# DVE's loads of expert numbers, POOL's fetches and the buffers of rows in two mixture-of-experts stages

## The reference

```python
def expert_block(args):
    xb, e = args
    hb = jax.nn.silu(xb @ w_gate[e]) * (xb @ w_up[e])
    return hb @ w_down[e]
```

## Time and profile before

| | |
|---|---|
| median of runs | 3517.16 us |
| profiled execution | 3516.36 us, span 3514.6 us |
| busy share of PE, DVE, ACT, POOL | 86%, 52%, 35%, 22% |
| mean granted clock of PE | 0.94 |
| DMA, mean over the span | 161 GB/s |

### The profile page before, as it was taken

How to read it: one execution, slowest core, us unless ns; L and a number is a source line. 1 busy time by engine, 2 the same in 40 slices (tenths; PEclk the granted TensorE clock), 3 DMA queues, 4 the chain that set the end, 5 groups by cost and what they waited for, 6 DMA issues and landing times. The chain is left out here.

```text
span 3514.6 us, 53911 instructions
## 1 busy us (share of the span) xinstructions
PE 3017.9 (86%) x17215; PEld 1423.1 (40%) x17216; DVE 1823.9 (52%) x2802; ACT 1212.8 (35%) x1768; POOL 761.8 (22%) x908
## 2 busy tenths in 40 slices
PE   8999999988999994788869997987888888888882
PEld 4444445545665443222247773444222222222220
DVE  3322224456774124333456674344677676776775
ACT  2221223334552001111133330211565555555564
POOL 1100000000000000434520000000555555555551
PEclk9999999998999996889979998999999999999996
DMA  6310021123221105888630101122778998888875
GB/s 227 125 66 30 0 102 49 54 57 84 73 73 60 68 36 201 332 346 347 225 142 25 36 27 66 63 102 104 268 242 290 333 331 277 304 286 274 281 236 180
DMA packets 188175, 564.40 MB, mean 161 GB/s; under 512 B 25340, under 2 KB 103776, under 8 KB 150912
## 3 DMA queue, kind: packets, MB, share of 16 engines
q1 hardware_dynamic: 146576, 425.10, 32.0%
q0 software_dynamic: 36528, 125.21, 13.6%
q10 hardware_dynamic: 4968, 12.74, 0.9%
HBM read 462.12 MB, written 100.86 MB: 160 GB/s over the span
## 5 line engine op out<-in xcount | busy, mean ns | idle before, releaser
L1467 POOL DMA_INDIRECT moe_xb<-token_rows,moe_idx x400 | 438.5, 1096 | 106.5 <-issue 93.0
L2137 DVE COPY h<-w_gu 128x1024 f32 (+1 forms) x342 | 267.0, 781 | 279.0 <-issue 238.7
L1561 POOL COPY moe_idx<-moe_slot_idx 128x4 int32<-128x4 int32 x4 | 0.6, 187 | 1814.6 <-DVE moe_slot_idx L1740 1814.6
L2030 PE MATMUL y_ps<-w_dn,hid_t 128*32 (+1 forms) x768 | 348.7, 597 | 11.1 <-issue 8.9
L2035 PE MATMUL y_ps<-h,hid_t 128*32 128x512 f32 (+1 forms) x768 | 348.7, 597 | 0.0
L362 PE MATMUL front<-second,wcol 128*128 128x512 f32 x768 | 332.1, 595 | 4.8 <-ACTq L68 2.4
L1999 PE MATMUL gu_ps<-w_gu,scores_mask 128*32 x576 | 278.8, 641 | 41.9 <-DVE more L2137 26.6
L2055 ACT ACTIVATE second<-w_gu 128x2048 f32 x146 | 271.0, 1903 | 98.6 <-issue 62.6
L1999 PE MATMUL gu_ps<-w_gu,more 128*32 x576 | 263.0, 611 | 48.7 <-DVE more L2125 16.3
L2004 PE MATMUL gu_ps<-second,scores_mask 128*32 128x512 f32 x576 | 278.9, 641 | 0.0
L2004 PE MATMUL gu_ps<-h,scores_mask 128*32 128x512 f32 x576 | 278.9, 641 | 0.0
(11 more groups left out here) (496 smaller groups left out, 6251.0 us busy)
## 6 DMA issues: line engine op xcount, KB each, us to landing
w_gu<-in_w_gate_dram SPq DMA_DIRECT2D x96, 1024.0 KB, 7.1
w_gu<-in_w_up_dram SPq DMA_DIRECT2D x96, 1024.0 KB, 11.0
w_dn<-in_w_down_dram SPq DMA_DIRECT2D x96, 1024.0 KB, 10.1
wcol<-in_w_in_dram SPq DMA_DIRECT2D x12, 1024.0 KB, 5.2
qk_by_head<-stage SPq DMA_DIRECT2D x32, 384.0 KB, 4.1
qk<-qk_by_head SPq DMA_DIRECT2D x16, 768.0 KB
expert_rows<-h ACTq DMA_DIRECT2D x24, 512.0 KB, 2.7
w_gu<-in_w_in_dram SPq DMA_DIRECT2D x20, 512.0 KB, 4.6
```

The source lines that it names most:

```text
L1467: g.indirect_dma_start(G.xb[:, slot % G.xb.shape[1], a, :], None, pieces, bass.IndirectOffsetOnAxis(ap=G.idx[:, slot, a:a + 1], axis=0)).t ...
L1561: g.tensor_copy(G.idx[:, b, :], G.slot_idx[:, b, :]).then_inc(idx_ready, 1)
L2030: nc.tensor.matmul(y_ps[0:SIZE, cs], hid_t[:, c, 0:SIZE], w_dn[:, bass.ds(ws, 1), c, cs].rearrange("p o n -> p (o n)"), start=c == 0, stop ...
L2137: d.tensor_copy(st_gu[a][:, :, cs, :], w_gu[:, bass.ds(ws, 1), :, cs, :].rearrange("p o g c n -> p (o g) c n")).then_inc(g_staged, 1)
```

## The change

Three things. DVE's step loads the expert numbers of block i+1 once and waits for their weights before it waits for `gu_ready`. POOL's iteration i now has `gather(i+2)` in front of `scatter(i-2)`, in both mixtures. And mixture 1 has two buffers for gathered rows and one for turned rows (instead of one and two): DVE turns the rows of block i+1 right behind `hid` of block i, since the one buffer is free only then; the dispatch stage gathers two blocks there, as it did for mixture 2. Cut to its core:

```diff
@@ dispatch, gpsimd
-            for b in range(G.xb.shape[1]):
+            for b in range(2):
                 gather_quads(g, G, rows_d, b)
@@ experts
         if more is None:
-            x_t = [rows.rearrange("p (c n) -> p c n", c=C) for rows in (work[:, 0], work[:, 1])]
+            x_t = [rows.rearrange("p (c n) -> p c n", c=C) for rows in (work[:, 0],)]
...
+        XT = len(x_t)
@@ experts, gpsimd
             def gather(b, slot):
-                pool.wait_ge(x_ready, b + 1 - XB)
+                pool.wait_ge(x_ready, b - 1)
                 if not by_slot:
-                    pool.wait_ge(share_ready, b + 1 - XB)
+                    pool.wait_ge(share_ready, b - 1)
...
-            for i in range(XB - 1, 4):
-                gather(i + 1, (i + 1) % 2)
+            for i in range(4):
+                gather(i + 2, i % 2)
                 if not by_slot and i >= 2:
                     scatter(i - 2, i % 2, None, 16 if i == 3 else None)
...
                     within.enter_context(pool.If(i <= n))
-                    gather(i + 1, 1 - u % 2)
+                    gather(i + 2, u % 2)
                     if not by_slot:
                         scatter(i - 2, u % 2, rounds + 16, rounds + (16 + 16 * (u % 2)))
@@ experts, vector
-            def stage_gate_up(b, pieces):
-                es = [v.value_load(G.blk_e[0:1, a, bass.ds(b, 1)], min_val=0, max_val=E - 1) for a in on_dve]
-                v.wait_ge(g_ready, es[-1] + 1)
-                if not (isinstance(b, int) and b == 0):
-                    v.wait_ge(gu_ready, b)
+            def experts_of(b):
+                return [v.value_load(G.blk_e[0:1, a, bass.ds(b, 1)], min_val=0, max_val=E - 1) for a in on_dve]
+
+            def stage_gate_up(es, pieces):
                 slots = [e % W for e in es]
...
             def step(i, turn, rounds):
                 slot = turn % 2
+                es = experts_of(i + 1)
+                v.wait_ge(g_ready, es[-1] + 1)
                 v.wait_ge(gu_ready, i + 1)
-                stage_gate_up(i + 1, (0,))
+                stage_gate_up(es, (0,))
                 v.wait_ge(silu_done, i + 1)
                 d.tensor_tensor(hid[:], act_g[:], gu_ps[:, slot, 1, :], ALU.mult).then_inc(hid_ready, 1)
-                stage_gate_up(i + 1, range(1, PIECES))
+                if XT == 1:
+                    v.wait_ge(x_in[1 - slot], (i + 1) // 2 * 64 + 64 if isinstance(i, int) else rounds * 4 + 128)
+                    turn_x(1 - slot)
+                stage_gate_up(es, range(1, PIECES))
                 stage_down(i)
-                v.wait_ge(x_in[slot], i // 2 * 64 + 128 if isinstance(i, int) else rounds * 4 + (128 + 64 * (1 - slot)))
-                turn_x(slot)
+                if XT == 2:
+                    v.wait_ge(x_in[slot], i // 2 * 64 + 128 if isinstance(i, int) else
+                              rounds * 4 + (128 + 64 * (1 - slot)))
+                    turn_x(slot)
@@ moe_state
-    G.xb = sb(f"moe_xb{E}", [P, lanes // 2, QUADS, width])
+    G.xb = sb(f"moe_xb{E}", [P, 2, QUADS, width])
@@ program
-            with nc.sbuf_tensor("work_1", [P, 2, D], F32) as work:
+            with nc.sbuf_tensor("work_1", [P, 1, D], F32) as work:
```

More of the change, by code:

```diff
@@ L1466, in gather_quads @@
     for a in range(QUADS):
-        g.indirect_dma_start(G.xb[:, slot % G.xb.shape[1], a, :], None, pieces, bass.IndirectOffsetOnAxis(
+        g.indirect_dma_start(G.xb[:, slot, a, :], None, pieces, bass.IndirectOffsetOnAxis(
             ap=G.idx[:, slot, a:a + 1], axis=0)).then_inc(G.xb_in[slot], 16)
@@ L1812, in experts @@
         xb, idx, mark = G.xb, G.idx, G.mark
-        XB = xb.shape[1]
         act_g = ph.sb("act_g", [P, F_EXP])
@@ L1921, in gather @@
             def gather(b, slot):
-                pool.wait_ge(x_ready, b + 1 - XB)
+                pool.wait_ge(x_ready, b - 1)
                 if not by_slot:
-                    pool.wait_ge(share_ready, b + 1 - XB)
+                    pool.wait_ge(share_ready, b - 1)
                 g.tensor_copy(idx[:, slot, :], G.slot_idx[:, bass.ds(b, 1), :].rearrange("p o a -> p (o a)")).then_inc(
                     idx_ready, 1)
-                pool.wait_ge(idx_ready, 2 * b + (1 - 2 * XB))
+                pool.wait_ge(idx_ready, 2 * b - 3)
                 g.tensor_tensor(mark[:, slot:slot + 1], G.tok[:, 0:1], G.tok[:, 0:1], ALU.add).then_inc(idx_ready, 1)
@@ L1974, in _ @@
                 pool.wait_ge(y_out_last, 16)
-            pool.wait_ge(x_in[0], (n + 3) // 2 * (16 * QUADS))
-            pool.wait_ge(x_in[1], (n + 2) // 2 * (16 * QUADS))
+            pool.wait_ge(x_in[0], (n + 4) // 2 * (16 * QUADS))
+            pool.wait_ge(x_in[1], (n + 3) // 2 * (16 * QUADS))
             if not by_slot:
-                pool.wait_ge(x_ready, n + 2)
+                pool.wait_ge(x_ready, n + XT)
                 pool.wait_ge(share_ready, n + 1)
@@ L1998, in step @@
                         pe.wait_ge(act_g_staged, 2 * i + (c * 2 // C + 1))
-                    nc.tensor.matmul(gu_ps[0:SIZE, slot], x_t[slot][:, c, 0:SIZE],
+                    nc.tensor.matmul(gu_ps[0:SIZE, slot], x_t[slot % XT][:, c, 0:SIZE],
                                      w_gu[:, bass.ds(ws, 1), :, c, :].rearrange("p o g n -> p (o g) n"),
@@ L2003, in step @@
                         at = slice(a * SIZE, (a + 1) * SIZE)
-                        last = nc.tensor.matmul(gu_ps[at, slot], x_t[slot][:, c, at], st_gu[a][:, :, c, :],
+                        last = nc.tensor.matmul(gu_ps[at, slot], x_t[slot % XT][:, c, at], st_gu[a][:, :, c, :],
                                                 start=c == 0, stop=c == C - 1)
@@ L2071, in take_share @@
                     e = a.value_load(G.blk_e[0:1, k, bass.ds(b, 1)], min_val=0, max_val=E - 1)
-                    last = s.activation(share[at, turn:turn + 1], xb[at, turn % XB, k, bass.ds(e + SUB, 1)], ACT.Copy)
+                    last = s.activation(share[at, turn:turn + 1], xb[at, turn % 2, k, bass.ds(e + SUB, 1)], ACT.Copy)
                 last.then_inc(share_ready, 1)
@@ L2124, in turn_x @@
             def turn_x(slot):
-                d.transpose(x_t[slot].rearrange("p c (a j) -> p a c j", j=QUARTER),
-                            xb[:, slot % XB, :, 0:SUB].rearrange("p a (i c) -> p a c i", c=C)).then_inc(x_ready, 1)
-            def stage_gate_up(b, pieces):
-                es = [v.value_load(G.blk_e[0:1, a, bass.ds(b, 1)], min_val=0, max_val=E - 1) for a in on_dve]
-                v.wait_ge(g_ready, es[-1] + 1)
-                if not (isinstance(b, int) and b == 0):
-                    v.wait_ge(gu_ready, b)
+                d.transpose(x_t[slot % XT].rearrange("p c (a j) -> p a c j", j=QUARTER),
+                            xb[:, slot, :, 0:SUB].rearrange("p a (i c) -> p a c i", c=C)).then_inc(x_ready, 1)
+            def experts_of(b):
+                return [v.value_load(G.blk_e[0:1, a, bass.ds(b, 1)], min_val=0, max_val=E - 1) for a in on_dve]
+            def stage_gate_up(es, pieces):
                 slots = [e % W for e in es]
@@ L2140, in stage_down @@
             def stage_down(b):
-                es = [v.value_load(G.blk_e[0:1, a, bass.ds(b, 1)], min_val=0, max_val=E - 1) for a in on_dve]
+                es = experts_of(b)
                 v.wait_ge(d_ready, es[-1] + 1)
@@ L2149, in step @@
                 slot = turn % 2
+                es = experts_of(i + 1)
+                v.wait_ge(g_ready, es[-1] + 1)
                 v.wait_ge(gu_ready, i + 1)
-                stage_gate_up(i + 1, (0,))
+                stage_gate_up(es, (0,))
                 v.wait_ge(silu_done, i + 1)
                 d.tensor_tensor(hid[:], act_g[:], gu_ps[:, slot, 1, :], ALU.mult).then_inc(hid_ready, 1)
-                stage_gate_up(i + 1, range(1, PIECES))
+                if XT == 1:
+                    v.wait_ge(x_in[1 - slot], (i + 1) // 2 * 64 + 64 if isinstance(i, int) else rounds * 4 + 128)
+                    turn_x(1 - slot)
+                stage_gate_up(es, range(1, PIECES))
                 stage_down(i)
-                v.wait_ge(x_in[slot], i // 2 * 64 + 128 if isinstance(i, int) else rounds * 4 + (128 + 64 * (1 - slot)))
-                turn_x(slot)
-            stage_gate_up(0, range(PIECES))
-            for b in range(2):
+                if XT == 2:
+                    v.wait_ge(x_in[slot], i // 2 * 64 + 128 if isinstance(i, int) else
+                              rounds * 4 + (128 + 64 * (1 - slot)))
+                    turn_x(slot)
+            es = experts_of(0)
+            v.wait_ge(g_ready, es[-1] + 1)
+            stage_gate_up(es, range(PIECES))
+            for b in range(XT):
                 v.wait_ge(x_in[b], 64)
@@ L2174, in moe_state @@
         G.m = sb(f"moe_m{E}", [P, T, E])[:]
-    G.slot_idx = sb(f"moe_slot_idx{E}", [P, NB + 5, QUADS], I32)[:]
+    G.slot_idx = sb(f"moe_slot_idx{E}", [P, NB + 6, QUADS], I32)[:]
     G.slot_row = sb(f"moe_slot_row{E}", [P, NB + 5], I32)[:] if lanes == 4 else None
```

## The result

The kernel after takes **3310.9 us** (median of 4 runs, 3308.1 to 3313.8) against 3517.5 for the one before on the same chip: ratio 0.9415, 95% interval 0.9398 to 0.9431. The profiled execution took 3308.1 us (span 3306.0).

The account below looks back on a forecast made before the run. DVE's late start behind register loads was taken to bound mixture 2, the only gather buffer mixture 1; -100 - 30 + 1 (additional gather) + 1.5 (tail) = -127.5 us, from 3517 to 3389 us, range 3335 to 3450.

Parts of the forecast that it names:

- term of -100 us for mixture 2: Mixture 2: mean period falls from 13.66 to 12.25 us over 71 blocks, DMA share then 0.93, -100 us.
- term of -30 for mixture 1: Mixture 1: second gather buffer removes the wait for rows, DMA then limits at a share of 0.94, -30 us.
- PE's floor is reached: Rival, both mixtures: DMA queues full at 0.98, -141 us in mixture 2, -45 in mixture 1, 3333 us; chance 0.18.
- PE's own period: Gate/up 7.07, hid's turn +3.37, next gate/up 0.96 to 1.40 later: 11.4 to 11.8 us a block at full clock.
- cap on DMA: Mixture 2: DMA engines busy 832 us; at 0.98 throughout the stage takes 849 us, a gain of 141; at 0.90, 66.
- signs of being wrong: Mixture 2: DVE's turns wait over 3 us for rows, loads over 1 us before the first copy, or DMA share stays 0.84.
- the 15 us that go by that rule: Mixture 1: at about 358 GB/s of HBM its 110 MB need 307 us, making the gain some 15 us smaller.
- the loads stay in the way: Rival: loads grow beside POOL's descriptor work, 1.5 of 2.78 us stays; -50 and -20 us, 3447 us; chance 0.10.
- Fetches are stretched by DVE's copies: Rival: POOL's gather issues slow beside DVE copies, gathers 5.3 us later; -47 and -25 us, 3445 us; chance 0.13.
- POOL ends last: Rival, slower: POOL's chain with five issues stretched by 1.3 us sets 15.2 us a block, +80 us, 3597; chance 0.04.
- later start of mixture 1: Before mixture 1: POOL issues four more gathers in front of the stage, so it starts 5 us later.
- the tail: End of mixture 2: a gather for a nonexistent block delays the last but one scatter, 0 to 6.2 us, taken as +1.5.

Follow-up runs that it names:

- number 8: Kernel after, but inside both mixture stages only the first half of each expert's down matrix is loaded: 3262.6 us, 0.9294 of before.
- number 7: Kernel after, but odd blocks' sums go into another table, so no scatter waits for the one before it: 3298.2 us, 0.9393 of before.
- number 1: Kernel before with only DVE's loads and wait for weights put in front of its wait for gate/up: 3438.0 us, 0.9788 of before.
- number 2: Kernel before with only mixture 2's gather put in front of the scatter, loads still behind the wait: 3414.6 us, 0.9722 of before.
- number 6: Kernel before, but in mixture 2 POOL holds each scatter, and the gather behind it, until the next gate/up ends: 3582.0 us, 1.0202 of before.
- number 5: Kernel before, but mixture 2's scatters, except the last, write rows instead of adding them: 3451.3 us, 0.984 of before.

## Why the prediction fell short

**The step that failed is the term of -100 us for mixture 2**: a mean period of 12.25 us, taken between PE's 11.6 and before with a DMA share of 0.93. Measured are 11.47 and -156 us. The term of -30 for mixture 1 was too small too, measured -48. No rival went as low either: "PE's floor is reached" had 3333. Two premises of the term were wrong, PE's own period and the cap on DMA. Of the prediction's signs of being wrong only single cases came (one turn that waited 5.8 us for rows, two of DVE's loads of over 1 us), and the DMA share rose to 0.95: the mechanism held, its size didn't.

**PE's own period: "7.07 + 3.37 + (0.96 to 1.40) = 11.4 to 11.8 us".** Measured are 10.87 in most of those 41 blocks of mixture 2, and 11.10 to 11.17 in 12 of mixture 1. The last term was read from a block in which hid came late and from one in which it came earlier, but not early enough. Once hid is ready, PE's sequencer sends hid's turn on to PE and then has register work for the next gate/up, the load of L1990 first. In the block of the earlier trace rows (before), and in the block shown after:

```profile
L1990 PEldq TENSOR_LOAD <-moe_blk_e x1: 298/298/298, 2907.7 to 2907.7; - x1
```
```profile
L1990 PEldq TENSOR_LOAD <-moe_blk_e x1: 298/298/298, 2600.4 to 2600.4; - x1
```

Both follow hid's end by 0.2 to 0.3 us. Before, the turn starts then too (2907.51), and the gate/up 1.40 behind it. After, the turn starts only behind the y products, at 2601.66, while the load of L1990 has begun at 2600.4: the register work goes on beneath the products, and the gate/up follows at +0.44. So the gap is near the larger of 3.80 and F + 3.1: blocks after with F of 1.41, 2.06 and 4.41 have gaps of 4.52, 5.15 and 7.50, a block before with 3.10 has 6.24 (a few lie up to 0.7 higher). Below an F of 0.7 nothing more is to be had, and that is where PE's period is 10.87. I had taken 1.40 (and 0.96) for PE's own; they were the exposed part of work that an early hid hides.

**The cap on DMA.** I held "832 us busy" for fixed work and chose 12.25 between PE and before, DMA share 0.93. After, the same bytes (335 GB/s x 823 us = 276 MB; before 280 x 990 = 277) took 0.95 x 823 = 782 busy us, 50 less. And a share can exceed 1 (1.02 over 200 us of mixture 1), so it sums the times of packets that overlap. It can't be divided by 0.98 to a floor: that gave 849 us for the stage, which took 814 from first to last gate/up. 11.47 lies inside what I had held for PE's own range; that is luck, since it is made of 10.87 in the undisturbed blocks and 0.6 on average of disturbance, mostly rows that come late. What is left above the floor is 71 x (11.47 - 10.87) = 43 us; number 8 gave back 29 of them, number 7 some 15.

**Mixture 1.** Forecast: last gate/up at 1709, -31; it came at 1692.7, -48. I took DMA at 0.94 (375 GB/s); it held 1.02 at 416 GB/s over 200 us. The Trainium skill's page "DMA: Bandwidth & Descriptors", section Specifications, gives about 358 GB/s of HBM for a core; here it doesn't hold over 200 of the stage's 288 us, and the 15 us that go by that rule were not lost. That DMA decides there was right: the waits for weights (48.7 us in 5) took the place of those for rows (200.3 in 23), and number 8, with a sixth fewer bytes, gave back 27 us there.

**The swap.** I valued it only by when the rows come, which is part of it (number 1 shows them late without it: 127 us of waits). But alone it gave -98, and DVE's loads are short with it (number 2). The forecast didn't need that, as the loads were moved too.

**What was right.** The hole was loads behind their wait; the first copy now starts within 0.4 us of gate/up's end in 34 of 72 blocks, and behind late rows in most others. Rivals: "the loads stay in the way" is refuted (17 long ones of 950, "issue" 5.4 us). "Fetches are stretched by DVE's copies" holds for single instructions: no gather issue in mixture 2 without a copy beside it takes over 1.04 us, before or after, and the one in the block above takes 1.42. The scatter's issue rose from a median of 1.65 us, with no copy beside it in any of 70, to 2.48, with copies beside 68 of 69. But the rival's price wasn't paid: it had 1.3 us for each gather issue, and their mean in mixture 2 went from 1.04 to 1.09. The Trainium skill's "SBUF — State Buffer", section SBUF: two separate sides, has POOL locked out for a copy's whole length. These durations lie between that and nothing: a scatter's issue after has copies beside it for 2.2 us on average and takes 0.8 longer. "POOL ends last" didn't come, though POOL is near it. The chain of waits after, from one scatter to the next, mixture 2 (start, us, what):

```profile
2591.48 11.02 DMA token_sums<-h,idx_y
...
2603.50 1.75 POOL token_sums L1943
...
2609.49 1.44 POOL moe_xb L1467
...
2614.45 0.39 POOL mark_y L1942
...
2614.98 10.96 DMA token_sums<-h,idx_y
```

Where the next scatter has to wait for it, which it does 51 times, a scatter now takes 11 us to land instead of a median of 6.4. The page's chain gives this DMA 6% of the span, some 200 us; number 7, which takes the wait away, won 8 to 15. A place in the chain is not a price. The later start of mixture 1 (+2.9, forecast +5) was sized well enough; the tail is 1.9 us shorter instead of 1.5 longer.

## What to carry to other kernels

A gap between two instructions, read where the producer was late, also holds the sequencer's own register work, which vanishes under queued work once the producer is early: take floors from blocks where nothing was late, and otherwise leave room below. A DMA share of busy time is no amount of work; here only the bytes stayed the same, and the rate rose. When register loads fill a hole, ask first why they are long: what runs just ahead of them may be as cheap to move as they are.

## What the runs showed of the hardware, unexpected

- A register load that takes 0.3 us takes up to 1.6 in some stretches behind an indirect DMA that adds: all 183 long loads before begin 2 to 4 us after its issue starts, in the queues of DVE (94), ACT (43), SP (42) and PE (4); the mean of all loads there is 0.91 and 1.01 us in the two microseconds. With a plain write the window is 1 to 3 us and 95 are long. Beside gathers in front of the scatter they stay at 0.3 (number 2). Neither the scatter alone (18 of 152 long in number 2) nor a gather close behind it (33 of 281 in number 6) is enough, and no run here separates a scatter's descriptors from its data: the cause stays open.
- One core held 416 GB/s over 200 us (mixture 1 after), with a DMA share of 1.02.
- A scatter's issue by POOL takes 1.65 us when it adds and 1.02 when it writes (medians, before and number 5), and 2.48 after, where it falls beside DVE's copies.
- PE's sequencer goes on with register work while PE works through queued matmuls: a gate/up follows 0.44 us behind hid's turn where hid was early, and 1.40 where it was late.
